# First layer's shift and scale summed by column groups, with values and gates accumulated by row tiles ahead of q and k

## The reference

```python
c_act = jax.nn.silu(c)
for i in range(DEPTH):
    shift, scale, gate = jnp.split(c_act @ mod_w[i] + mod_b[i], 3, axis=-1)
    h = _rms_norm(x, norm_g[i]) * (1.0 + scale[:, None, :]) + shift[:, None, :]
    ...
    x = x + gate[:, None, :] * y

q, k, v, g = jnp.split(h @ w_in, [RET_DK, 2 * RET_DK, 2 * RET_DK + RET_DV], axis=-1)
q = _rope(q, positions) * (RET_HK ** -0.5)
k = _rope(k, positions)
...
o = _layer_norm(o)
return (o * jax.nn.silu(g)) @ w_out
```

## Time and profile before

| | |
|---|---|
| median of 3 runs | 755.2 us (753.25 to 755.22) |
| the profiled execution | 753.32 us, of which the span of the profile 751.5 us |
| PE busy | 714.9 us, 95% |
| DVE busy | 510.8 us, 68% |
| ACT busy | 376.2 us, 50% |
| HBM read | 137.3 MB, 184 GB/s over the span |

### The profile page before, as it was taken

One profiled execution on the slowest core, in us unless ns is written; L12 is line 12 of the kernel. 1 busy time (PEld: TensorE's weight loads), 2 busy tenths in 40 slices (PEclk: granted clock), 3 DMA queues, 4 the chain that ended last, 5 costly groups with the idle time before them and its releaser, 6 DMA issues.

```text
span 751.5 us, 9325 instructions
## 1 busy us (share of the span) xinstructions
PE 714.9 (95%) x3527; PEld 587.6 (78%) x3527; DVE 510.8 (68%) x705; ACT 376.2 (50%) x555; POOL 21.5 (3%) x35
## 2 busy tenths in 40 slices
PE   0899999999999899999999999999999999999996
PEld 0878878778788678888887788877887888888884
DVE  6888968887686755645567789955575556555444
ACT  2274435545544747554555654534556453544343
POOL 5000000000000000000001100000000000000000
PEclk9999999999999999999999999999999999999998
DMA  9986668777687344533255553432365656655521
GB/s 325 400 271 226 232 217 271 258 242 235 227 310 253 108 167 146 167 125 101 91 174 156 168 168 105 122 97 97 117 197 191 182 183 191 185 186 185 192 70 57
DMA packets 67404, 138.95 MB, mean 185 GB/s; under 512 B 5730, under 2 KB 8144, under 8 KB 67360
## 3 DMA queue, kind: packets, MB, share of 16 engines
q1 hardware_dynamic: 65632, 134.82, 54.3%
q0 software_dynamic: 848, 1.57, 0.8%
q10 hardware_dynamic: 880, 1.97, 0.8%
HBM read 137.30 MB, written 1.05 MB: 184 GB/s over the span
## 4 chain that ended last, share of the span: by engine, by line
PE 87%; DVE 7%; ACT 3%; issue 2%; DMA 1%; ACTq 0%; DVEq 0%
PE G L329 24%; PE G L331 23%; PE G L330 23%; PE T L350 4%; PE T L616 3%; PE T L645 2%; PE T L740 2%; DVE wlo L917 1%; DVE arena L926 1%; DVE arena L917 1%; DVE arena L921 1%; ACT gate L1646 1%; PE G L392 1%; PE T L538 1%; DVE x L917 1%
## 5 line engine op out<-in xcount | busy, mean ns | idle before, releaser
L917 DVE TENSOR_TENSOR wlo<-raw,whi 128x1024 fp32r<-128x1024 f32 x206 | 250.5, 1223 | 141.7 <-ACT whi L1644 140.3
L329 PE MATMUL G<-whi,ahi 128*128 128x512 f32 x824 | 332.7, 404 | 5.2 <-DVE wlo L917 4.3
L331 PE MATMUL G<-whi,alo 128*128 128x512 f32 x824 | 322.6, 391 | 0.0
L330 PE MATMUL G<-wlo,ahi 128*128 128x512 f32 x824 | 321.7, 390 | 0.0
L1644 ACT ACTIVATE whi<-raw 128x1024 fp32r<-128x1024 f32 x206 | 217.3, 1059 | 129.3 <-PE G L331 128.7
L329 PEld LDWEIGHTS G<-whi,ahi 128*128 128x128 f32 x824 | 155.3, 188 | 40.8 <-DVE wlo L917 8.7
L331 PEld LDWEIGHTS G<-whi,alo 128*128 128x128 f32 x824 | 154.9, 188 | 33.8
L330 PEld LDWEIGHTS G<-wlo,ahi 128*128 128x128 f32 x824 | 155.5, 189 | 30.5 <-issue 1.0
L926 DVE SCALAR_TENSOR_TENSOR acc<-raw,cact,acc 128x1024 f32<-128x1024 f32 x32 | 41.0, 1281 | 2.0
L350 PE MATMUL T<-head,arena 128*128 128x128 f32 x212 | 32.9, 284 | 7.9 <-DVE arena L921 7.0
L1646 ACT ACTIVATE arena<-T,st 128x128 f32<-128x128 f32 (+1 forms) x48 | 16.9, 419 | 46.5 <-DVE st L1273 46.5
(11 more groups left out here) (194 smaller groups left out, 515.9 us busy)
## 6 DMA issues: line engine op xcount, KB each, us to landing
raw<-in_mod_w_dram SPq DMA_DIRECT2D x48, 512.0 KB, 5.3
raw<-in_ret_w_in_dram SPq DMA_DIRECT2D x48, 512.0 KB, 5.2
raw<-in_w_gate_up_dram SPq DMA_DIRECT2D x40, 512.0 KB, 3.6
raw<-in_fox_w_in_dram SPq DMA_DIRECT2D x32, 512.0 KB, 4.4
raw<-in_w_in_dram SPq DMA_DIRECT2D x28, 512.0 KB, 3.6
raw<-in_w_down_dram SPq DMA_DIRECT2D x22, 512.0 KB, 4.4
raw<-in_ret_w_out_dram SPq DMA_DIRECT2D x16, 512.0 KB, 5.2
raw<-in_fox_w_out_dram SPq DMA_DIRECT2D x8, 512.0 KB, 3.9
```

The costliest lines, as they stand in the source:

```text
L329: e.matmul(o, ah, wh, start=first and k == 0, stop=False)
L330: e.matmul(o, ah, wl, start=False, stop=False)
L331: done = e.matmul(o, al, wh, start=False, stop=last and k == 1)
L917: e.tensor_tensor(o, a, b, op).then_inc(sig[name], 1)
```

## The change

The first layer's shift and scale are no longer 16 items ahead of all units. SP loads x first, then `mod_w` in five column groups of 128, 128, 256, 256 and 256 columns (shift and scale together, all 1024 rows, in an arena of their own), with units between the groups. DVE sums 7 of 8 row tiles of a group, PE adds the eighth and sums over partitions; this gives `AB` for one or two of the eight feature tiles of h at a time (`shift_scale`, `modulated`). ACT and DVE then make `ahi` and `alo` of that feature tile (`x0_high`, `x0_low`).

The units that come first are those of v of heads 0 and 1 and g of head 0. They accumulate by row tiles, so that each needs just the feature tiles made so far: a v unit is one row tile by 1024 columns (`rows_unit`, four G banks), a g unit two row tiles by 512 columns in banks T0 and T1. After these 12 units come q and k (units 12 to 27), then g of head 1, v and g of heads 2 and 3 (units 28 to 47). The rope angles move from the start to behind units 12 to 14. The mod items of the second layer's shift and scale and of the first gate (24) follow units 12 and later by `j * 15 // 8`; the 8 of the second gate move into the second layer, with `gate_rows(1)`, whose sum is kept in `gate[:, 1, :]`. The transposes that nothing reads between the layers become 32. POOL zeroes `acc` once two items are used, instead of at once. Signals are merged and renamed; that is left out here.

```diff
+    out = []
+    for k in range(0, 8, 2):
+        out += [("w", [(rows_of(W0, 2048, 1024, k + i, 1), 0)], 1024) for i in range(2)]
+        out.append(("w", [(rows_of(W0, 4096, 512, k, 2), 0)], 512))
     main = [u for c in range(4) for u in chunk(W0, 512 * c)]
-    for h in range(4):
-        main += chunk(W0, 2048 + 512 * h) + chunk(W0, 4096 + 512 * h)
-    main += outer(ret_w_out, 16)
-    mods = [mod(1, k, c0) for k in range(8) for c0 in (0, D)]
-    mods += [mod(layer, k, 2 * D) for layer in range(2) for k in range(8)]
+    for c0 in (4096 + 512, 2048 + 1024, 4096 + 1024, 2048 + 1536, 4096 + 1536):
+        main += chunk(W0, c0)
+    main += outer(ret_w_out, 16, (1, 0))
+    mods = [mod(1, k, c0) for k in range(8) for c0 in (0, D)] + [mod(0, k, 2 * D) for k in range(8)]
     after = {}
-    for j in range(32):
-        n = 4 * j + 3 if j < 4 else 16 + (j - 4) * 8 // 5 if j < 24 else 51 + (j - 24) * 4 // 3
-        after.setdefault(n, []).append(mods[j])
-    out = [mod(0, k, D * half) for half in range(2) for k in range(8)]
+    for j in range(24):
+        after.setdefault(j * 15 // 8, []).append(mods[j])
     for n, u in enumerate(main):
         out += [u, *after.get(n, [])]
-    for c in range(8):
-        out += chunk(W1, 512 * c)
-        if c == 0:
+    fox = [u for c in range(8) for u in chunk(W1, 512 * c)]
+    for n, u in enumerate(fox):
+        out.append(u)
+        if n == 3:
             out.append(("f", [(rows_of(W1, 4096, 16, 0, 8), 0)], 16))
+        if 4 <= n < 20 and n % 2 == 0:
+            out.append(mod(1, (n - 4) // 2, 2 * D))
...
+SUMMED = [(0,), (1,), (2, 3), (4, 5), (6, 7)]
...
+            def turn_x0(k):
+                on_.wait_ge(sig["xn"], 2 if k < 4 else 4)
+                on_.wait_ge(sig["h_in"], k - 1)
+                transposes(T[2 + k % 2], [xn0[:, m, k * P:(k + 1) * P] for m in range(2)], "x0_turned")
...
+            def shift_scale(g):
+                for i, n in mod_in[g]:
+                    on_.wait_ge(sig[f"mod_in{i}"], n)
+                for i, k in enumerate(SUMMED[g]):
+                    for a in range(2):
+                        o = T[2 + k % 2][:, 256 + a:257 + a]
+                        e.matmul(o, raw0[:, a, 7, i * P:(i + 1) * P], cact[:, 7:8], start=True, stop=False)
+                        on_.wait_ge(sig["macc"], g + 1)
+                        d = e.matmul(o, sums[:, a, i * P:(i + 1) * P], ones[:, 0:1], start=False, stop=True)
+                    d.then_inc(sig["sums"], 1)
+                    for m in range(2):
+                        ready[k, m] = (sig["x0"], k + 1)
+            def rows_unit(u, k):
+                on_.wait_ge(sig["used"], item_of[u] + 1)
+                on_.wait_ge(*ready[k, 0])
+                j = u % NH
+                for c in range(2):
+                    wh, wl = whi[:, j, c * 512:(c + 1) * 512], wlo[:, j, c * 512:(c + 1) * 512]
+                    for m in range(2):
+                        ah, al = ahi[:, k, m * P:(m + 1) * P], alo[:, k, m * P:(m + 1) * P]
+                        o = G[2 * c + m][:, :]
+                        e.matmul(o, ah, wh, start=k == 0, stop=False)
+                        e.matmul(o, ah, wl, start=False, stop=False)
+                        done = e.matmul(o, al, wh, start=False, stop=k == 7)
+                    done.then_inc(sig["g"], 1)
+                    products_n[0] += 1
+                    done_at[u, c] = products_n[0]
+            turn_x0(0)
+            shift_scale(0)
+            turn_x0(1)
+            rows_unit(0, 0)
+            shift_scale(1)
+            on_.wait_ge(sig["rows_read"], 3)
+            for k in range(0, 8, 2):
+                u = 3 * (k // 2)
+                if k:
+                    rows_unit(u, k)
+                rows_unit(u + 1, k + 1)
+                if k < 6:
+                    turn_x0(k + 2)
+                    turn_x0(k + 3)
+                products(u + 2, 0, (4, 5, None), k, k == 0, k == 6)
+                if k < 6:
+                    shift_scale(2 + k // 2)
+                products(u + 2, 1, (4, 5, None), k, k == 0, k == 6)
...
             t = bank("warm", sig["warm"], 1)
-            for n in range(16):
+            for n in range(32):
...
+                elif k == 3:
+                    gate_rows(1, GATE1, gate[:, 1, :])
...
+            def mod_sums(g, r0, r1):
+                raw0, o = mod_tile(g), macc[:, g % 2, :, 0:P * len(SUMMED[g])]
+                on_.wait_ge(sig["cact"], 1)
+                on_.wait_ge(sig["sums"], (0, 0, 1, 2, 4)[g])
+                for r in range(r0, r1):
+                    i, n = mod_in[g][r // 4 if len(SUMMED[g]) > 1 else 0]
+                    on_.wait_ge(sig[f"mod_in{i}"], n)
+                    on_.wait_ge(sig["mod_sum"], mod_n[0] if r else 0)
+                    a = raw0[:, :, r, :]
+                    name = "macc" if r == 6 else "mod_sum"
+                    mod_n[0] += r < 6
+                    if r == 0:
+                        ts(o, a, col(cact, 0), None, ALU.mult, None, name)
+                    else:
+                        stt(o, a, col(cact, r), o, ALU.mult, ALU.add, name)
...
+            def modulated(k):
+                t = T[2 + k % 2]
+                on_.wait_ge(sig["sums"], k + 1)
+                on_.wait_ge(sig["columns"], 3)
+                tt(AB[:, 0, 8 + k:9 + k], t[:, 256:257], mbc[:, k:k + 1], ALU.add, "mod0")
+                ts(AB[:, 0, k:k + 1], t[:, 257:258], mb1[:, k:k + 1], g_col[:, 0, k:k + 1], ALU.add, ALU.mult, "mod0")
...
+            ts(st[:, 0:2], st[:, 0:2], 1.0 / D, EPS, ALU.mult, ALU.add, "rms")
+            mod_sums(0, 0, 2)
+            on_.wait_ge(sig["rms_act"], 1)
+            e.reciprocal(st[:, 0:2], st[:, 0:2]).then_inc(sig["rms"], 1)
+            mod_sums(0, 2, 7)
+            modulated(0)
+            ring_to(0)
+            x0_low(0)
+            mod_sums(1, 0, 7)
+            modulated(1)
+            ring_to(1)
+            tt(n1f[:, :], t[:, 70:78], n1_col, ALU.mult, "rows_read")
+            x0_low(1)
+            ring_to(2)
+            for g in (2, 3, 4):
+                k, u = 2 * g - 2, 3 * g - 3
+                mod_sums(g, 0, 4)
+                if g > 2:
+                    ring_to(u - 1)
+                mod_sums(g, 4, 7)
+                modulated(k)
+                modulated(k + 1)
+                ring_to(u)
+                x0_low(k)
+                ring_to(u + 1)
+                x0_low(k + 1)
+            ring_to(11)
...
+            def x0_high(k):
+                on_.wait_ge(sig["x0_turned"], k + 1)
+                on_.wait_ge(sig["mod0"], 2 * k + 2)
+                on_.wait_ge(sig["x0"], k - 3)
+                act(stage0[:, k % 4, :], T[2 + k % 2][:, 0:256], ACT.Identity, "h_in", scale=col(AB[:, 0, :], k), bias=col(AB[:, 0, :], 8 + k))
+                on_.wait_ge(sig["h_in"], k + 1)
+                act(ahi[:, k, :], stage0[:, k % 4, :], ACT.Copy, "h_hi")
+            normal(0)
+            ring_to(0)
+            x0_high(0)
+            normal(4)
+            ring_to(1)
+            x0_high(1)
+            ring_to(2)
+            ring_to(3)
+            x0_high(2)
+            x0_high(3)
+            ring_to(5)
+            for k in (4, 6):
+                ring_to(3 * k // 2 + 1)
+                x0_high(k)
+                x0_high(k + 1)
+                ring_to(3 * k // 2 + 2)
+            ring_to(12)
...
+            values_of(0, done_at[10, 0], 0)
+            ring_to(13)
+            values_of(1, done_at[10, 1], 1)
+            on_.wait_ge(sig["g"], done_at[11, 1])
+            gates_of(0, T[0:2])
+            ring_to(14)
...
+            on_.wait_ge(sig["used"], 2)
             fill(acc[:, :], 0.0, "acc_zero")
...
+            on_.wait_ge(sig["rope"], 32)
+            fill(gate[:, 1, :], 0.0, "acc_zero")
+            on_.wait_ge(sig["acc_zero"], 2)
+            e.dma_start(gate[0:1, 1, :], mod_b[1:2, 2 * D:3 * D]).then_inc(sig["acc_in"], 16)
...
+            def load_mod(g):
+                n, o = P * len(SUMMED[g]), mod_tile(g)
+                on_.wait_ge(sig["mod0"], (0, 0, 0, 4, 8)[g])
+                for part in range(len(SUMMED[g])):
+                    r0, nr = 4 * part, 8 // len(SUMMED[g])
+                    for a in range(2):
+                        e.dma_start(o[:, a, r0:r0 + nr, :], rows_of(mod_w[0], D * a + P * SUMMED[g][0], n, r0, nr)).then_inc(sig[f"mod_in{mod_in[g][part][0]}"], 16)
+            before = {0: 0, 1: 1, 3: 2, 6: 3, 9: 4}
+            for m in range(2):
+                e.dma_start(x[:, m, :], x_in[0, m * P:(m + 1) * P, :]).then_inc(sig[f"x_in{m}"], 16)
             for n, (_, srcs, w, *_) in enumerate(items):
+                if n in before:
+                    load_mod(before[n])
                 t = raw_tile(n)
```

509 lines of the change are left out of this document (223 added, 286 removed).

## The result

| | before | the change |
|---|---|---|
| median of 20 runs each | 753.4 us | 756.9 us |
| lowest, highest | 752.8, 756.7 | 753.2, 758.4 |
| profiled execution, span | 751.5 | 754.8 |

The ratio is 1.003, with a 95% interval of 1.0017 to 1.0044: slower by about the 0.3% that can be told from no change, where 0.2% faster was forecast. (These 20 runs of before have a lower median than the three that the prediction had.)

A forecast was written before the change was run, and what follows sets the result against it. PE was taken to bound the kernel behind the start, something else in the start. Gains of 3.9 by unit 57, less 1.75 and 0.7 between layers, gave 1.4: span 751.5 to 750.1, plus 1.8, 752 us; range 745 to 759.

The forecast's parts named there:

- which the change leaves alone: The long stretch behind 250 us: PE-bound, unchanged by the change, so nothing else there was worth costing.
- The start: Up to unit 12: unit 0 at 15.9 us, unit 12 at 63.5 against 72.8 to compare, a gain of 9.3.
- PE's answer 0.6: In each start group's chain, PE's reply to DVE's sums takes 0.6 us, within cycles of 9.5 or 10.7.
- some 2 us in each: In the three start groups of two tiles, PE waits some 2 us each, needing 8.2 for its units.
- The sums of 512 columns: DVE's sums in the two-tile start groups: 0.72 us each, 0.82 with the dependence, bounds 0.53 and 1.40.
- The zeroing by POOL: In the start, POOL's zeroing of acc holds DVE's passes during the sums: 1.0 us, bounds 0 and 2.7.
- Given back: Units 12 to 57: mod items behind the ropes delay wlo, giving back 5.8 us, bounds 0 and 9.3.
- The three terms 2.9, 0.9 and 1.9: Waits given back: first q and k chunk 2.9 us, two later chunks 0.9, last rope near unit 31 1.9.
- Between the layers: Between the layers: gate_rows(1) moved to where PE never waits costs 1.75 us, 32 transposes instead of 16 cost 0.7.
- The third rival: The clock falls in PE's pauses before the start's groups: four pauses, +5.6 us, 757.5; chance 0.09.
- the second rival: Start groups' loads in narrow rows arrive late, DVE waits, kernel slower: 5 us taken, 757; chance 0.14.

The follow-up runs named there:

- e9: The changed kernel with PE's part of a group's sums ahead of its wait for DVE's part; units 3 to 12 took 31.31 us.
- e10: e8 with e9's order of the sums and the last 16 mod items of the first layer spread evenly; 748.2 us, 0.9922 of the kernel before.
- e5: The changed kernel with four mod items moved from directly behind a rope to one unit earlier or later; units 12 to 57 took 154.26 us instead of 156.21.
- e13: The changed kernel with only the second head group's logits moved behind unit 126; 754.3 us, 1.0005 of the kernel before.
- e14: The kernel before with only the second head group's logits moved behind unit 126; 753.9 us, ratio 1.0001.
- e1: The kernel before with 18 transposes that nothing reads ahead of the logits in the first two groups; 755.3 us.
- e7: The changed kernel with unread transposes in PE's start pauses, 11 of them ahead of the wait for the small vectors; unit 12 at 67.42 us.
- e8: The changed kernel with e5's table (first three items earlier), e7's filling, second gate's sum and items back, 16 transposes between layers; 748.8 us, 0.9930.
- e11: e10 with the logits of the second head group one unit later, on all engines; 747.0 us, 0.9908 of the kernel before.

## Why the prediction was wrong

Two things went wrong. The forecast was 1.4 us gained, and at unit 84 it should have been seen whole; there the change is 0.1 ahead. And behind it the step "which the change leaves alone" failed, by which 3.0 us were lost. The steps, by the table:

- **The start, 9.3 forecast, 5.6 measured** (74.74 - 67.19 - 1.92 for the turns). Unit 0 was right to 0.4, unit 1 to 0.5, and the wait of 2.55 for tile 1's sums, behind a unit 0 at half clock, was foreseen (shift and scale near 22, measured 22.16). The step that failed is "PE's answer 0.6" in the three groups of two tiles: DVE waited for PE's sums 4.9 us in them (two waits in each, of 0.92 or 1.37 and of 0.55), where the forecast has 1.8. All such waits of the changed kernel, 14 to 67 us, and three of them in the timeline of DVE, with one for ACT:

```profile
DVE AB L970 <- PE T L418: 8.1, 8, 2.5
...
22.16 0.16 DVE L970 TENSOR_TENSOR AB<-T,mbc 128x1 f32<-128x1 f32 x1 [2.55 <-PE T L418]
...
33.25 0.16 DVE L970 TENSOR_TENSOR AB<-T,mbc 128x1 f32<-128x1 f32 x1 [0.55 <-PE T L418]
...
35.76 1.23 DVE L970 TENSOR_TENSOR wlo<-raw,whi 128x1024 fp32r<-128x1024 f32 x1 [0.70 <-ACT whi L1718]
...
44.82 0.16 DVE L970 TENSOR_TENSOR AB<-T,mbc 128x1 f32<-128x1 f32 x1 [1.37 <-PE T L418]
```

  The wait at 33.25 is for the second tile's four small products, which had no term in the sum, and the one at 44.82 for half a unit that stands ahead on PE and then for the first tile's products. Those 3.1 us are most of the 3.7 that are missing; the 0.70 for ACT's `whi` had no term either. A pair's eight products take PE 1.7 (55.04 to 56.77), and the earlier trace rows had the price: 1.92 for the eight of L395, recorded as 16. PE waited 0.4 to 0.5 before the first unit of each of these groups, not "some 2 us in each". e9 shows that the order of the small products among themselves is not the cause, as the group stays at 11.2 where 10.7 was forecast. The sums of 512 columns were near: 0.79 for one with its dependence, forecast 0.82 (4.76 for six, below). The clock has a share too. From unit 1 to unit 12 the change took 43.0 and the forecast has 39.8; e10, where the clock stayed up and e9's order gives 0.2, took 41.6. So some 1.2 of these 3.2 are falls, and 1.8 are there without any. That e10's whole way from unit 0 to 12, 47.8, is nearly the forecast's 47.6 is luck, since the forecast has unit 0 at half clock in it.
- **The zeroing by POOL**, taken at 1.0 (0 to 2.7), cost 0.35. The one-operand pass of DVE took 0.83 against 0.48 in the next groups, and ended 0.3 behind the zeroing; the `wlo` beside it took its usual 1.22:

```profile
23.70 2.66 POOL L2221 MEMSET acc<- 128x3072 f32 x1 [15.13 <-DVE wlo L970]
...
24.67 1.22 DVE L970 TENSOR_TENSOR wlo<-raw,whi 128x1024 fp32r<-128x1024 f32 x1 [0.52 <-ACT whi L1718]
25.81 0.83 DVE L974 TENSOR_SCALAR arena<-arena,cact 128x512 f32<-128x512 f32 x1
26.67 4.76 DVE L979 SCALAR_TENSOR_TENSOR arena<-arena,cact 128x512 f32<-128x512 f32 x6
```

  This is what "SBUF — State Buffer" of the Trainium skill says in "SBUF: two separate sides", that a pass with two operands in SBUF contends only with a GpSimd operation that reads SBUF, which a zeroing doesn't; going by the rule, with 0 to 1.0 for its sum, would have been nearer.
- **Given back, 5.8 forecast, 3.8 measured** (156.2 - 150.5 - 1.9). The mechanism was right: e5 took 1.95 of it away by moving four items. The first rope was less late than forecast (a wait of 0.8 for it and not 1.9). The three terms 2.9, 0.9 and 1.9 make 5.7, written as 5.8.
- **Between the layers, 2.45 forecast, 1.8 measured**: 0.55 for the transposes (forecast 0.7; the per-transpose price was 0.11, as 1.91 for 16 in the earlier trace rows says, and not the 0.055 written) and 1.25 for the gate's sum (1.75, since its four matmuls take 1.88 by their modelled ends and 1.3 by their spacing).
- **Behind 250 us, "which the change leaves alone"**: this is the step that turned the sign. The code there is the same, but not the clock: two falls at the logits, 3.0 us from unit 120 to 130, and with the logits apart (e13) the change is level with the kernel before, 1.0005. The third rival had the mechanism, the clock, in the wrong place and at 0.09. It had also the falls in the start, which came: the clock was at one half from 14 to 21, 24 to 28 and 34 to 38 us. What they cost is within the 5.6.
- **Narrow loads** were not late. While the groups were read, from 16 to 67 us, DMA moved 318 GB/s at a share of 0.92, and no sum waited for a transfer (only the very first sum did, 0.53 at 9.76 us), so the second rival did not come:

```profile
16.00:67.00 51.00, 46.51 (x212) 38.07 (x213) 39.28 (x68) 22.96 (x34) 4.23 (x4) 0.89 0.92 318
```

**Left open**: why the change meets the falls at the logits more often. Up to unit 120 both kernels are at the same time to 0.3 us in their profiles, so it is hardly how late the stretch comes. The start differs: its clock falls in every profile with the change's start unfilled, and in one of four with the start of before. That this is the cause is not shown. "TensorE: Matmul & The Clock Gate" of the Trainium skill says in Part 1 that the gate's observation isn't reset when a kernel starts, by which one would expect the falls to come about as often in both; the runs here, 23 of 32 against 8 of 92, don't look so, and no run here shows how a start could act on a stretch 450 us later. A version of the kernel before with a start made idle was not tried.

## To carry to other kernels

Move work between two places only with the price in each: a sum that fills a wait is free, and costs its whole time in a stretch where the engine never waits. Read a change of a few tenths of a per cent by distances between the same two instructions in several profiles, own repeats included, before any of it is put down to an edit. And list the stretches of small products that bring the clock down in some runs: setting a unit of large matmuls between two of them cost nothing that could be told here (e14) and took 2.4 us from the change. A sum that goes back and forth between two engines needs a term for each engine's part in it, priced by a row.

## What the runs showed of the hardware

- The granted clock takes 1.7 us of full clock at a time here, or twice or three times that: 1.55 us longer for each where PE is the bound, about 1 us in the start of the change, where DVE's chain hides part, 0.6 in that of e1. Timed runs of one program lie in groups 1.3 to 3.5 us apart for it, each with its own mean granted clock (0.986, 0.982 and 0.980 for the change).
- The clock fell at 495.3 us behind small products, though PE was busy for 5.94 of the 6 us from 490 to 496 by the profile.
- Where no fall comes, a stretch of 45 units (12 to 57) repeats to 0.1 us over versions and runs (156.11 to 156.21 in eight profiles with the same code there).
- Transposes in a pause did not keep the clock up reliably: the same filling had the clock down from 13 to 20 us in e7 and e8, from 16 to 19 in e11 and never in e10.
